# SwiGLU feed-forward on one core: three instead of four ordinary pairs of units ahead of the seven-product pairs, and a new order for the operands of the first of these

## The chip, the cores and the metric

One NeuronCore of a Trainium2 chip runs the whole program in one launch. The metric is the device time of that core in microseconds. The kernel before takes 2061.83 us, the median of three runs (2058.19 to 2067.65).

## What is computed

One inference step of a four-layer decoder trunk for 512 prompt tokens and 8 sample tokens, 520 columns in all. The layers have the mixers pool, conv, attention and pool, and each is followed by a feed-forward, which is where the change lies:

```python
def swiglu(h, w_gate, w_up, w_down):
    return (jax.nn.silu(h @ w_gate) * (h @ w_up)) @ w_down

xp = xp + swiglu(rmsnorm(xp, norm_ffn[i]), ffn_w_gate[i], ffn_w_up[i], ffn_w_down[i])
```

The model's width is 1024 (8 tiles of 128) and the feed-forward's 2816 (22 tiles of 128, numbered f). All is float32. The kernel computes each product as three: the operands are split into a high part (rounded to the engine's fp32r) and a low part (the rest), and hi\*hi + hi\*lo + lo\*hi are summed.

## The kernel before

Five engines run five programs written out by hand, in `@block.tensor`, `@block.scalar`, `@block.vector`, `@block.gpsimd` and `@block.sync`. Each goes through its own list in order; semaphores alone tie them together. There is no scheduler: the order of the Python code is the order on the engine. The gate weights of one f (128 columns of `w_gate`) and the up weights of the same f make a pair, and there are two ways to multiply it by the 520 tokens:

- **Ordinary** (`unit` on TensorE, the first PLAIN = 4 values of f of each layer, so 8 units). A unit is 8 input tiles by 2 token halves by 3 products, 48 matmuls of 260 columns, 96 for gate and up. Its weights are split by ScalarE (`split`, L1312, `w_hi`) and VectorE (`split`, L1817, `w_lo`). VectorE takes gate and up out of PSUM times `rstd` (L2009 `gate_n`, L2027 `up`), ScalarE takes silu (L1470), VectorE multiplies (L2036 `h`), and `h` is split too (`h_high` L1460, `h_low` L1999).
- **Seven-product** (`seven_blocks` on TensorE, L871, the other 18 values of f). Gate and up by the two halves of the inputs are a 2 by 2 matrix of blocks, and the halves of the inputs by the two halves of the tokens another; their product is made of seven block products instead of eight. A block is 4 input tiles by 3 products, 12 matmuls of 260 columns, 84 for a pair. It costs sums of operands: of weights on VectorE (`w_sum_2`, three sums, L1977 to L1980, and `w_sum_4`, one, L1988), each block's weights split (`high(j, b)` on ScalarE, L1455; `low(j, b)` on VectorE, L1994, 128x512 each), and, once a layer, sums and splits of the normed inputs: `scaled` (L1958, 16 instructions), four sums `xt` (L2025) and seven splits of 128x1040, `x_high(b)` (L1444) and `x_low(b)` (L1967), one for each block b of every pair. The results are joined (`join` on both engines): ScalarE copies the running bank out after blocks 0, 2 and 4 (L1502 `begun`), and TensorE must wait for the copies before blocks 2, 4 and 6, because these go on summing in the same bank (`pe.wait_ge(begun_ok, 3 * J + 1)` and so on; J counts pairs over the layers). VectorE adds the copies to other banks (L2057 to L2066), ScalarE takes silu of the halves (L1492, L1495), and VectorE makes `h` (L2070, L2071).

In the steady state the weights of pair j + 1 are split during pair j, and the first three sums of pair j + 2 are made after block 5 of pair j. The first pair has no pair before it: its operands, and the seven splits of the inputs, are made while TensorE is in the ordinary units. A layer runs the ordinary units, seven-product pairs up to f = 10, the first half of the down product, eleven more pairs, and the second half of it. SyncE loads weights into four places `raw`; a load waits until what lay there was split. On ScalarE and VectorE the loop `for c in range(PLAIN)` orders all this, and after it `join`. In ScalarE's `join(0)`:

```python
if b == 3:
    act.wait_ge(joined, 4 * J + 1)
    act.activation(silu2[:, 0:HALF], silu2[:, 0:HALF], ACT.Silu)
```

comes ahead of the copy after block 4, and so, in the same list, do the splits of the next pair's blocks 0 to 3 (`ahead(b)` stands behind each b).

Of the kernel before, what the change touches and what calls it, by code (L numbers as in the profile page):

```python
# [34 lines left out]
KT = D // P  # L35
# [17 lines left out]
PLAIN = 4  # L53
# [150 lines left out]
def trunk_step(nc, x_prompt, x_sample, state_pool, state_conv, cache_k, cache_v, page_table,  # L204
# [7 lines left out]
    with ctx:  # L212
# [1084 lines left out]
        def _(act):  # L1297
# [130 lines left out]
            def ffn(layer):  # L1428
# [32 lines left out]

                for c in range(PLAIN):
                    n, f = At(u + 2 * c), FT * layer + c
                    if c + 1 < PLAIN:
                        split(n + 2)
                    else:
                        for b in range(3):
                            high(0, b)
                    act.wait_ge(evacuated, m0 + 2 * c + 1)
                    act.activation(silu2[:], gate_n[:], ACT.Silu).then_inc(sg_ready, 1)  # L1470
                    if c + 1 < PLAIN:
                        split(n + 3)
                    else:
                        for b in (3, 4):
                            high(0, b)
                        x_high(4)
                        act.wait_ge(units_done, u + 2 * PLAIN)
                        for b in (5, 6):
                            x_high(b)
                            high(0, b)  # L1480
                    if c + 1 < PLAIN:
                        h_high(c)
                    for b in ((1, 2, 3) if c + 2 == PLAIN else (0,) if c + 3 == PLAIN else ()):
                        x_high(b)

                def join(j, ahead, last):

                    J, f = PAIRS * layer + j, PLAIN + j
                    for b in range(7):
                        if b == 3:  # L1490
                            act.wait_ge(joined, 4 * J + 1)
                            act.activation(silu2[:, 0:HALF], silu2[:, 0:HALF], ACT.Silu)  # L1492
# [3 lines left out]
                        act.wait_ge(blk_done, 7 * J + b + 1)  # L1496
                        if b in (0, 2, 4):
                            if J:
                                act.wait_ge(joined, 4 * J - 3 + b // 2)
                            if j == 0 and b == 0:  # L1500
                                act.wait_ge(sg_ready, FT * layer + PLAIN)
                            act.activation(begun[b // 2][:], pair[:, J % 2, 0:HALF], ACT.Copy).then_inc(begun_ok, 1)  # L1502
# [300 lines left out]
        def _(dve):  # L1803
# [142 lines left out]
            def ffn(layer):  # L1946
# [54 lines left out]
                for c in range(PLAIN):  # L2001
                    n, f = At(u + 2 * c), FT * layer + c
                    if c + 1 == PLAIN:
                        w_sum_2(0)
                        w_sum_4(0)
                    dve.wait_ge(units_done, n.start + 1)
                    if c:
                        dve.wait_ge(sg_ready, f)
                    dve.tensor_tensor(halves(gate_n[:]), accumulator(At(0)), halves(rstd[:]), ALU.mult).then_inc(evacuated, 1)  # L2009
                    if c + 1 < PLAIN:  # L2010
                        split(n + 2)
                    else:
                        for b in range(4):
                            low(0, b)
                    if c == 0:
                        for k in range(4):
                            scaled(k)
                    if c == 1:
                        dve.wait_ge(x_scaled, layer + 1)
                        dve.wait_ge(stored, 16 * STORED[("pool0", "conv", "attn", "pool1")[layer]])  # L2020
                        for to, a, b, made in ((xt[:, 0], xn1[:, 0:4], xn0[:, 0:4], 0), (xt[:, 1], xn1[:, 4:8], xt[:, 0], 1),
                                         (xt3[:], xn0[:, 4:8], xt[:, 1], 2), (xt[:, 2], xn1[:, 4:8], xn1[:, 0:4], 0)):
                            if made:
                                dve.wait_ge(x_summed, 4 * layer + made)
                            dve.tensor_tensor(to, a, b, ALU.subtract).then_inc(x_summed, 1)  # L2025
                    dve.wait_ge(units_done, n.start + 2)
                    dve.tensor_tensor(halves(up2[:]), accumulator(At(1)), halves(rstd[:]), ALU.mult).then_inc(evacuated, 1)  # L2027
                    if c + 1 == PLAIN:
                        low(0, 4)
                        x_low(4)  # L2030
                        for b in (5, 6):
                            x_low(b)
                            low(0, b)
                    dve.wait_ge(sg_ready, f + 1)
                    dve.wait_ge(evacuated, m0 + 2 * c + 2)
                    dve.tensor_tensor(h2[:], up2[:], silu2[:], ALU.mult).then_inc(h_ready, 1)  # L2036
                    if c + 1 < PLAIN:
                        split(n + 3)
                        h_low(c)
                    else:  # L2040
                        w_sum_2(1)
                    if c == 0:
                        for k in range(4, KT):
                            last = scaled(k)
                        last.then_inc(x_scaled, 1)
                    for b in ((1, 2, 3) if c + 2 == PLAIN else (0,) if c + 3 == PLAIN else ()):
                        x_low(b)
# [589 lines left out]
```

## Time and profile before

| | |
|---|---|
| median of three runs | 2061.83 us |
| the profiled execution, its own time | 2060.63 us |
| its span, first to last instruction | 2058.8 us |
| busy: TensorE, VectorE, ScalarE, GpSimd | 1999.7, 1414.7, 1055.4, 254.4 us |
| TensorE clock granted, mean | 0.995 of full |

The busy time of TensorE counts overlapped matmuls once. One matmul of 260 columns is shown with about 283 ns, but they are pipelined: the next starts about 120 ns after it, so work on TensorE is counted by starts. On VectorE and ScalarE too an instruction often starts a little before the one ahead has ended, and the step from start to start is what an instruction costs in a full queue.

### The profile page before, as it was taken

Reading aid. Unit: us, or ns where it says so; the run is one execution under the profiler, and the core shown is the slowest. Engines: PE = TensorE matmul, PEld = TensorE weight load, DVE = VectorE, ACT = ScalarE, POOL = GpSimd, SP = SyncE. Lnnn points to the kernel's source line nnn. Section 1 sums busy time; section 2 is a strip of 40 time slices with the busy share of each in tenths; the row PEclk is TensorE's granted clock in tenths of the full one; section 3 lists DMA queues with packets and bytes.
Section 4 is the critical chain, followed back from the end, with each engine's and each line's share of the span. In section 5 each row is a group of like instructions: output and inputs, shape, how many; then the busy total and the mean of one; then the engine's idle time right before and its main releaser. Section 6 shows DMA issues by size and latency. Waiting matters only on the chain.

```text
span 2058.8 us, 41713 instructions
## 1 busy us (share of the span) xinstructions
PE 1999.7 (97%) x16672; PEld 1933.2 (94%) x16672; DVE 1414.7 (69%) x2410; ACT 1055.4 (51%) x1842; POOL 254.4 (12%) x253
## 2 busy tenths in 40 slices
PE   8999999999899999999999979999999999999999
PEld 7999999997599999999999859999999999999999
DVE  5994696568768946964566655795597269937952
ACT  5553464465455534653777753463365355624642
POOL 4000000169320000001111124000000120000001
PEclk9999999999999999999999999999999999999999
DMA  6233333344222333333532342233333323333332
GB/s 187 74 103 97 98 104 100 89 119 119 64 73 72 103 93 102 103 98 95 177 114 82 108 180 84 84 83 99 96 108 99 109 62 87 97 92 110 103 97 79
DMA packets 350021, 208.22 MB, mean 101 GB/s; under 512 B 9897, under 2 KB 340553, under 8 KB 349812
## 3 DMA queue, kind: packets, MB, share of 16 engines
q1 hardware_dynamic: 345988, 198.26, 33.2%
q0 software_dynamic: 3472, 6.96, 1.0%
q8 instruction: 121, 1.98, 0.4%
q10 hardware_dynamic: 384, 0.55, 0.1%
q14 instruction: 56, 0.46, 0.1%
HBM read 194.53 MB, written 8.60 MB: 99 GB/s over the span
## 4 chain that ended last, share of the span: by engine, by line
PE 80%; DVE 9%; POOL 4%; issue 3%; ACT 3%; DMA 1%; SPq 0%; POOLq 0%; DVEq 0%; ACTq 0%
PE acc L671 41%; PE pair L871 19%; PE acc L871 9%; PE bank L871 4%; POOL conv L2540 4%; PE pair L1080 1%; DVE w_lo L1817 1%; PE bank L1100 1%; DMA hist_rows<-in_state_pool 1%; DVE w_lo L1994 1%; DVE xn L1958 1%; PE pair L1055 1%; DVE pair L2167 1%; ACT w_hi L1312 1%; DVE xt_lo L1967 1%
## 5 line engine op out<-in xcount | busy, mean ns | idle before, releaser
L1312 ACT ACTIVATE w_hi<-raw 128x768 fp32r<-128x768 f32 (+1 forms) x220 | 199.4, 906 | 439.3 <-PE acc L671 436.1
L671 PE MATMUL acc<-h_hi,w_hi 128*128 128x260 f32 x1408 | 399.0, 283 | 0.0
L671 PE MATMUL acc<-h_lo,w_hi 128*128 128x260 f32 x1408 | 398.3, 283 | 0.0
L671 PE MATMUL acc<-h_hi,w_lo 128*128 128x260 f32 x1408 | 397.7, 282 | 0.0
L1817 DVE TENSOR_TENSOR w_lo<-raw,w_hi 128x768 fp32r<-128x768 f32 (+1 forms) x220 | 241.9, 1099 | 216.3 <-ACT w_hi L1312 210.9
L671 PE MATMUL acc<-xin_hi,w_hi 128*128 128x260 f32 x1152 | 332.5, 289 | 6.0 <-DVE w_lo L1817 4.8
L671 PE MATMUL acc<-xin_hi,w_lo 128*128 128x260 f32 x1152 | 326.2, 283 | 0.0
L671 PE MATMUL acc<-xin_lo,w_hi 128*128 128x260 f32 x1152 | 325.7, 283 | 0.0
L671 PEld LDWEIGHTS acc<-h_hi,w_hi 128*128 128x128 f32 x1408 | 265.2, 188 | 0.3
L671 PEld LDWEIGHTS acc<-h_hi,w_lo 128*128 128x128 f32 x1408 | 265.1, 188 | 0.0
L671 PEld LDWEIGHTS acc<-h_lo,w_hi 128*128 128x128 f32 x1408 | 264.8, 188 | 0.0
L671 PEld LDWEIGHTS acc<-xin_hi,w_hi 128*128 128x128 f32 x1152 | 217.5, 189 | 20.5 <-issue 13.9
L671 PEld LDWEIGHTS acc<-xin_lo,w_hi 128*128 128x128 f32 x1152 | 217.6, 189 | 0.2
L671 PEld LDWEIGHTS acc<-xin_hi,w_lo 128*128 128x128 f32 x1152 | 217.5, 189 | 0.0
L1455 ACT ACTIVATE w_hi<-w_sum 128x512 fp32r<-128x512 f32 x216 | 132.8, 623 | 31.3 <-PE acc L871 20.5
L1994 DVE TENSOR_TENSOR w_lo<-w_sum,w_hi 128x512 fp32r<-128x512 f32 x216 | 147.3, 684 | 0.6
L1502 ACT ACTIVATE begun<-pair 128x260 f32<-128x260 f32 x216 | 82.8, 383 | 94.0 <-PE pair L871 93.0
L2452 POOL COPY sqacc<-sq 128x520 f32<-128x520 f32 x7 | 5.5, 782 | 961.2 <-ACT sq L1318 961.2
L1994 DVE TENSOR_TENSOR block<-raw,block 128x512 fp32r<-128x512 f32 x140 | 95.8, 687 | 39.2 <-ACT block L1455 38.5
L871 PE MATMUL pair<-xn_hi,block 128*128 128x260 f32 x576 | 114.9, 282 | 0.0
L871 PE MATMUL pair<-xt_hi,block 128*128 128x260 f32 x544 | 109.4, 284 | 0.0
L871 PE MATMUL bank<-xn_hi,block 128*128 128x260 f32 x544 | 109.2, 282 | 0.0
(445 smaller groups left out, 5264.9 us busy)
## 6 DMA issues: line engine op xcount, KB each, us to landing
raw<-in_ffn_w_gate SPq DMA_DIRECT2D x88, 512.0 KB, 4.0
raw<-in_ffn_w_up SPq DMA_DIRECT2D x88, 512.0 KB, 5.2
raw<-in_ffn_w_down SPq DMA_DIRECT2D x64, 384.0 KB, 3.5
raw<-in_ffn_w_down SPq DMA_DIRECT2D x64, 320.0 KB, 3.2
raw<-in_attn_w_qkv SPq DMA_DIRECT2D x24, 512.0 KB, 3.9
raw<-in_conv_w_in SPq DMA_DIRECT2D x16, 512.0 KB, 4.1
raw<-in_conv_w_out SPq DMA_DIRECT2D x8, 512.0 KB, 4.3
in_mix<-in_cache_k SPq DMA_DIRECT2D x8, 512.0 KB, 5.3
```

Of the source, the lines that this page charges most:

```text
L671: last = pe.matmul(acc[:, b, 0:HALF], w[:, w_tile * P:(w_tile + 1) * P], v[:, h * HALF:(h + 1) * HALF], start=start and t == 0, stop=stop ...
L871: last = pe.matmul(block_bank(J, b), w[:, cols], v[:, k, :], start=k + t == 0 and b in (0, 1, 3, 5), stop=k == 3 and t == 2, skip_group_ch ...
L1055: last = pe.matmul(pair[:, t, 0:HALF], blk, sq[:, 0, t * HALF:(t + 1) * HALF], start=True, stop=True)
L1080: last = pe.matmul(pair[:, c, off:off + w], qn[c * QK:(c + 1) * QK, i * P:(i + 1) * P], kn[c * QK:(c + 1) * QK, 0:w], start=True, stop=True)
L1100: last = pe.matmul(bank7[:, i * P:(i + 1) * P], aT[:, off + j * P:off + (j + 1) * P], v_tok[:, g % 2, j, :], start=j == 0, stop=j == i)
L1312: act.activation(w_hi[n.slot(2)][:, 0:cols], raw[:, q.slot(4), 0:cols], ACT.Copy).then_inc(split_hi, 1)
L1455: act.activation(block_w(j, b)[0], block_of(b, q), ACT.Copy).then_inc(blk_hi, 1)
L1502: act.activation(begun[b // 2][:], pair[:, J % 2, 0:HALF], ACT.Copy).then_inc(begun_ok, 1)
L1817: dve.tensor_tensor(w_lo[n.slot(2)][:, 0:cols], raw[:, raw_of(n).slot(4), 0:cols], w_hi[n.slot(2)][:, 0:cols].bitcast(F32), ALU.subtract). ...
L1958: last = dve.scalar_tensor_tensor(to[:, k, :], x[:, k, cols], g, rstd[:, cols], ALU.mult, ALU.mult)
L1994: dve.tensor_tensor(lo, block_of(b, raw_of_pair(layer, j)), hi.bitcast(F32), ALU.subtract).then_inc(blk_lo, 1)
L2540: pool_e.tensor_tensor(out, out, prod_p[:, p % 3, :], ALU.add).then_inc(prod_added, 1)
```

## The change

PLAIN becomes 3, so f = 3 is made by a seven-product pair too: 6 units, 8 pairs, down, 11 pairs, down. On VectorE and ScalarE the loop's conditionals are written out, and the operands of the first pair are made block by block: the input's split, the weights' split, then those of the next block. On ScalarE the copy of the bank after block 0 of the first pair is put ahead of the splits for blocks 5 and 6; in every pair silu of the first half moves from ahead of the copies of b = 3 to behind the copy after block 4. On VectorE the splits of the second pair's blocks 0 and 1 are made ahead of `join` rather than in it.

```diff
-PLAIN = 4
+PLAIN = 3
...
+                def copy_begun(J, b):
+
+                    act.wait_ge(blk_done, 7 * J + b + 1)
...
+                    act.activation(begun[b // 2][:], pair[:, J % 2, 0:HALF], ACT.Copy).then_inc(begun_ok, 1)
...
                     else:
-                        for b in range(3):
-                            high(0, b)
+                        x_high(0)
+                        high(0, 0)
                     act.wait_ge(evacuated, m0 + 2 * c + 1)
                     act.activation(silu2[:], gate_n[:], ACT.Silu).then_inc(sg_ready, 1)
...
+                x_high(1)
+                high(0, 1)
+                x_high(2)
+                high(0, 2)
+                x_high(3)
+                high(0, 3)
+                high(0, 4)
+                x_high(4)
+                act.wait_ge(units_done, u + 2 * PLAIN)
+                x_high(5)
+                copy_begun(PAIRS * layer, 0)
+                high(0, 5)
+                x_high(6)
+                high(0, 6)
...
                     for b in range(7):
-                        if b == 3:
-                            act.wait_ge(joined, 4 * J + 1)
-                            act.activation(silu2[:, 0:HALF], silu2[:, 0:HALF], ACT.Silu)
...
+                        if b == 4:
+                            act.wait_ge(joined, 4 * J + 1)
+                            act.activation(silu2[:, 0:HALF], silu2[:, 0:HALF], ACT.Silu)
...
+                gate_up(1, 1, up2)
+                h_of(1)
+                split(At(u + 5))
+                h_low(1)
+                x_low(0)
+                low(0, 0)
+                gate_up(2, 0, gate_n)
+                x_low(1)
+                low(0, 1)
+                w_sum_2(0)
+                x_low(2)
+                low(0, 2)
+                gate_up(2, 1, up2)
+                x_low(3)
+                low(0, 3)
+                w_sum_4(0)
+                x_low(4)
+                low(0, 4)
+                x_low(5)
+                low(0, 5)
+                h_of(2)
+                x_low(6)
+                low(0, 6)
+                low(1, 0)
+                low(1, 1)
+                w_sum_2(1)
...
-                            if not last:
+                            if not last and (j or b > 1):
                                 low(j + 1, b)
```

How the lists move, at the places that the prediction speaks of. The lines of the changed file are some numbers higher: in it L1976 is `x_low`, L2003 `low`, L2015 `gate_n` and `up`, L2021 `h`, L1986 to L1997 the sums of weights. The numbers behind names are the program's own: `block_83`, `early_86` and `early_87` hold the weights of blocks 0, 1 and 2, `w_lo_59` and `w_lo_60` of an ordinary unit or of blocks 3 and 4, 5 and 6; `xn_lo`, `xt_lo` and `late_lo` are the inputs' low parts.

VectorE in the first layer, the kernel before, from the first `x_low`:

```order
L1967 TENSOR_TENSOR xn_lo<-xn_79,xn_hi 128x1040
L2009 TENSOR_TENSOR gate_n<-acc,rstd 128x520
L1817 TENSOR_TENSOR w_lo_59<-raw,w_hi_57 128x1024
L2027 TENSOR_TENSOR up_101<-acc,rstd 128x520
L2036 TENSOR_TENSOR h_102<-up_101,silu_99 128x520
L1817 TENSOR_TENSOR w_lo_60<-raw,w_hi_58 128x1024
L1999 TENSOR_TENSOR h_lo<-h_102,h_hi 128x520
L1967 TENSOR_TENSOR xn_lo<-xn_79,xn_hi 128x1040
L1967 TENSOR_TENSOR xt_lo<-xt,xt_hi 128x1040 x2
L1977 TENSOR_TENSOR w_sum<-raw 128x512
L1978 TENSOR_TENSOR w_sum<-raw 128x512
L1980 TENSOR_TENSOR w_sum<-w_sum,raw 128x512
```

and the change, from the same place:

```order
L1976 TENSOR_TENSOR xn_lo<-xn_79,xn_hi 128x1040
L2003 TENSOR_TENSOR block_83<-raw,block_83 128x512
L2015 TENSOR_TENSOR gate_n<-acc,rstd 128x520
L1976 TENSOR_TENSOR xn_lo<-xn_79,xn_hi 128x1040
L2003 TENSOR_TENSOR early_86<-raw,early_86 128x512
L1986 TENSOR_TENSOR w_sum<-raw 128x512
L1987 TENSOR_TENSOR w_sum<-raw 128x512
L1989 TENSOR_TENSOR w_sum<-w_sum,raw 128x512
L1976 TENSOR_TENSOR xt_lo<-xt,xt_hi 128x1040
L2003 TENSOR_TENSOR early_87<-w_sum,early_87 128x512
L2015 TENSOR_TENSOR up_101<-acc,rstd 128x520
L1976 TENSOR_TENSOR xt_lo<-xt,xt_hi 128x1040
```

The two splits of ordinary weights have gone, and the first pair's operands begin right behind the first `x_low`.

VectorE at the start of the first `join`, the kernel before:

```order
L1994 TENSOR_TENSOR w_lo_60<-raw,w_hi_58 128x512
L2036 TENSOR_TENSOR h_102<-up_101,silu_99 128x520
L1977 TENSOR_TENSOR w_sum<-raw 128x512
L1978 TENSOR_TENSOR w_sum<-raw 128x512
L1980 TENSOR_TENSOR w_sum<-w_sum,raw 128x512
L1994 TENSOR_TENSOR block_83<-raw,block_83 128x512
L1988 TENSOR_TENSOR w_sum<-raw,w_sum 128x512
L2057 TENSOR_TENSOR silu_99<-bank,begun_95 128x260
```

and the change:

```order
L2003 TENSOR_TENSOR w_lo_60<-raw,w_hi_58 128x512
L2003 TENSOR_TENSOR block_83<-raw,block_83 128x512
L2003 TENSOR_TENSOR block_92<-raw,block_92 128x512
L1986 TENSOR_TENSOR w_sum<-raw 128x512
L1987 TENSOR_TENSOR w_sum<-raw 128x512
L1989 TENSOR_TENSOR w_sum<-w_sum,raw 128x512
L1997 TENSOR_TENSOR w_sum<-raw,w_sum 128x512
L2078 TENSOR_TENSOR silu_99<-bank,begun_95 128x260
```

The second pair's sums of weights now stand behind two of its splits.

ScalarE from the last ordinary silu to the first copy of the bank, before:

```order
L1470 ACTIVATE silu_99<-gate_n 128x520
L1455 ACTIVATE w_hi_57<-w_sum 128x512 x2
L1444 ACTIVATE xt_hi<-xt 128x1040
L1444 ACTIVATE late_hi<-xn_88 128x1040
L1455 ACTIVATE w_hi_58<-w_sum 128x512
L1444 ACTIVATE late_hi<-xt_89 128x1040
L1455 ACTIVATE w_hi_58<-raw 128x512
L1502 ACTIVATE begun_95<-pair 128x260
```

and the change:

```order
L1479 ACTIVATE silu_99<-gate_n 128x520
L1444 ACTIVATE xn_hi<-xn_79 128x1040
L1455 ACTIVATE early_86<-raw 128x512
L1444 ACTIVATE xt_hi<-xt 128x1040
L1455 ACTIVATE early_87<-w_sum 128x512
L1444 ACTIVATE xt_hi<-xt 128x1040
L1455 ACTIVATE w_hi_57<-w_sum 128x512 x2
L1444 ACTIVATE xt_hi<-xt 128x1040
L1444 ACTIVATE late_hi<-xn_88 128x1040
L1469 ACTIVATE begun_95<-pair 128x260
```

The copy is ahead of three splits that it followed, but four splits that were made before the last silu now stand behind it and ahead of the copy.

## Rows read from the trace of the kernel before

**Rows 1.** The page, part 1: busy time, share of the span and instructions.

```profile
PE 1999.7 (97%) x16672; PEld 1933.2 (94%) x16672; DVE 1414.7 (69%) x2410; ACT 1055.4 (51%) x1842; POOL 254.4 (12%) x253
```

**Rows 2.** TensorE's waits: us in total, times, longest us.

```profile
PE pair L871 <- ACT begun L1502: 13.7, 12, 1.6
```

**Rows 3.** The chain that ended last: start us, us, what.

```profile
1414.86 63.42 PE acc L671 x528
```

**Rows 4.** Timeline of TensorE, first layer: start us, us, what [idle before <-releaser].

```profile
77.94 0.39 PE L671 MATMUL acc<-xin_hi,w_hi 128*128 128x260 f32 x1 [0.78 <-DVE w_lo L1817]
...
95.28 0.28 PE L871 MATMUL pair<-xn_hi,block 128*128 128x260 f32 x1
...
99.83 0.39 PE L871 MATMUL pair<-xt_hi,early 128*128 128x260 f32 x1 [1.51 <-ACT begun L1502]
...
107.41 0.39 PE L871 MATMUL pair<-late_hi,w_hi 128*128 128x260 f32 x1 [1.55 <-ACT begun L1502]
...
115.25 0.38 PE L871 MATMUL pair<-xt_hi,w_hi 128*128 128x260 f32 x1 [0.39 <-ACT begun L1502]
```

**Rows 5.** Timeline of VectorE, first layer.

```profile
56.90 0.70 DVE L2009 TENSOR_TENSOR gate_n<-acc,rstd 128x520 f32<-128x520 f32 x1 [0.41 <-ACT rstd L1333]
...
78.41 1.24 DVE L1967 TENSOR_TENSOR xn_lo<-xn,xn_hi 128x1040 fp32r<-128x1040 f32 x1
79.57 0.69 DVE L2009 TENSOR_TENSOR gate_n<-acc,rstd 128x520 f32<-128x520 f32 x1
...
84.00 0.70 DVE L2027 TENSOR_TENSOR up<-acc,rstd 128x520 f32<-128x520 f32 x1 [2.61 <-PE acc L671]
...
90.64 0.69 DVE L1977 TENSOR_TENSOR w_sum<-raw 128x512 f32<-128x512 f32 x1
91.25 0.69 DVE L1978 TENSOR_TENSOR w_sum<-raw 128x512 f32<-128x512 f32 x1
...
103.88 0.69 DVE L1980 TENSOR_TENSOR w_sum<-w_sum,raw 128x512 f32<-128x512 f32 x1
```

**Rows 6.** Timeline of ScalarE, first layer.

```profile
80.30 0.64 ACT L1470 ACTIVATE silu<-gate_n 128x520 f32<-128x520 f32 x1 [0.97 <-DVE gate_n L2009]
...
87.05 2.02 ACT L1444 ACTIVATE xt_hi<-xt 128x1040 fp32r<-128x1040 f32 x2
...
99.42 0.36 ACT L1502 ACTIVATE begun<-pair 128x260 f32<-128x260 f32 x1
99.69 1.14 ACT L1455 ACTIVATE block<-raw 128x512 fp32r<-128x512 f32 x2
...
104.60 0.64 ACT L1455 ACTIVATE block<-w_sum 128x512 fp32r<-128x512 f32 x1 [1.17 <-DVE w_sum L1980]
```

**Rows 7.** Timelines, second and fourth layer: VectorE's first `gate_n`, TensorE's first block 6.

```profile
623.08 0.70 DVE L2009 TENSOR_TENSOR gate_n<-acc,rstd 128x520 f32<-128x520 f32 x1 [3.38 <-ACT rstd L1333]
...
674.66 0.39 PE L871 MATMUL pair<-late_hi,w_hi 128*128 128x260 f32 x1 [1.54 <-ACT begun L1502]
...
1699.10 0.70 DVE L2009 TENSOR_TENSOR gate_n<-acc,rstd 128x520 f32<-128x520 f32 x1 [3.02 <-ACT rstd L1333]
...
1749.51 0.39 PE L871 MATMUL pair<-late_hi,w_hi 128*128 128x260 f32 x1 [1.52 <-ACT begun L1502]
```

**Rows 8.** The page, part 6: a load's size in KB and median us to landing.

```profile
raw<-in_ffn_w_up SPq DMA_DIRECT2D x88, 512.0 KB, 5.2
```

**Rows 9.** Windows: us; busy of PE, PEld, DVE, ACT, POOL; PEclk, DMA share, GB/s.

```profile
242.00:340.00 98.00, 98.00 (x820) 98.00 (x819) 88.22 (x170) 61.94 (x124) 0.00 (x0) 1.00 0.37 102
...
484.00:487.40 3.40, 3.40 (x16) 3.40 (x17) 2.75 (x4) 1.66 (x3) 3.26 (x3) 0.50 0.38 89
487.40:490.80 3.40, 3.40 (x30) 3.40 (x29) 2.63 (x2) 1.52 (x3) 3.26 (x3) 0.99 0.67 178
```

**Rows 10.** Timeline of TensorE, conv mixer, ahead of the window at 484.00.

```profile
483.93 0.52 PE L671 MATMUL acc<-xin_hi,w_hi 128*128 128x260 f32 x1 [2.08 <-DVE w_lo L1817]
484.25 0.42 PE L671 MATMUL acc<-xin_lo,w_hi 128*128 128x260 f32 x1
484.46 0.42 PE L671 MATMUL acc<-xin_hi,w_lo 128*128 128x260 f32 x1
```

More of the change, by code:

```diff
@@ L1460, in h_high @@
                     act.activation(h_hi[:, f % FH, :], h2[:], ACT.Copy).then_inc(h_hi_ok, 1)
+                def copy_begun(J, b):
+                    act.wait_ge(blk_done, 7 * J + b + 1)
+                    if J:
+                        act.wait_ge(joined, 4 * J - 3 + b // 2)
+                    if J == PAIRS * layer and b == 0:
+                        act.wait_ge(sg_ready, FT * layer + PLAIN)
+                    act.activation(begun[b // 2][:], pair[:, J % 2, 0:HALF], ACT.Copy).then_inc(begun_ok, 1)
                 for c in range(PLAIN):
@@ L1472, in ffn @@
                         split(n + 3)
[L1473 to L1481, printed above, removed]
-                        h_high(c)
-                    for b in ((1, 2, 3) if c + 2 == PLAIN else (0,) if c + 3 == PLAIN else ()):
-                        x_high(b)
+                        h_high(c)
+                x_high(1)
[12 more added lines that the diff above has]
+                high(0, 6)
                 def join(j, ahead, last):
@@ L1495, in join @@
                             act.activation(silu2[:, HALF:T], silu2[:, HALF:T], ACT.Silu).then_inc(sg_ready, 1)
[L1496 to L1502, printed above, removed]
+                        if b in (0, 2, 4) and j + b:
+                            copy_begun(J, b)
+                        else:
+                            act.wait_ge(blk_done, 7 * J + b + 1)
+                        if b == 4:
+                            act.wait_ge(joined, 4 * J + 1)
+                            act.activation(silu2[:, 0:HALF], silu2[:, 0:HALF], ACT.Silu)
                         if b == (0 if j else 2) and j != PAIRS_OF[1][0]:
@@ L1999, in h_low @@
                     dve.tensor_tensor(h_lo[:, f % FH, :], h2[:], h_hi[:, f % FH, :].bitcast(F32), ALU.subtract).then_inc(h_lo_ok, 1)
[L2001 to L2034, printed above, removed]
@@ L2035, in ffn, with gate_up, h_of @@
+                def gate_up(c, j, to):
+                    dve.wait_ge(units_done, u + 2 * c + j + 1)
+                    if c and j == 0:
+                        dve.wait_ge(sg_ready, FT * layer + c)
+                    dve.tensor_tensor(halves(to[:]), accumulator(At(j)), halves(rstd[:]), ALU.mult).then_inc(evacuated, 1)
+                def h_of(c):
+                    dve.wait_ge(sg_ready, FT * layer + c + 1)
                     dve.wait_ge(evacuated, m0 + 2 * c + 2)
                     dve.tensor_tensor(h2[:], up2[:], silu2[:], ALU.mult).then_inc(h_ready, 1)
[L2037 to L2047, printed above, removed]
+                gate_up(0, 0, gate_n)
+                split(At(u + 2))
+                for k in range(4):
+                    scaled(k)
+                gate_up(0, 1, up2)
+                h_of(0)
@@ new lines, in ffn @@
+                split(At(u + 3))
+                h_low(0)
+                for k in range(4, KT):
+                    last = scaled(k)
+                last.then_inc(x_scaled, 1)
+                gate_up(1, 0, gate_n)
+                split(At(u + 4))
+                dve.wait_ge(x_scaled, layer + 1)
+                dve.wait_ge(stored, 16 * STORED[("pool0", "conv", "attn", "pool1")[layer]])
+                for to, a, b, made in ((xt[:, 0], xn1[:, 0:4], xn0[:, 0:4], 0), (xt[:, 1], xn1[:, 4:8], xt[:, 0], 1),
+                                 (xt3[:], xn0[:, 4:8], xt[:, 1], 2), (xt[:, 2], xn1[:, 4:8], xn1[:, 0:4], 0)):
+                    if made:
+                        dve.wait_ge(x_summed, 4 * layer + made)
+                    dve.tensor_tensor(to, a, b, ALU.subtract).then_inc(x_summed, 1)
```

## The prediction

> **What bounds the kernel now.** I read the page first: TensorE is busy 97% of the span [rows 1], so a change counts by what it does to TensorE's list. Then TensorE's waits: the longest line is twelve waits for `begun`, 13.7 us [rows 2], three in the first pair or two of each of the four layers. The chain gives TensorE's pace: 528 matmuls in 63.42 us, 0.12 us each [rows 3], so a block is 1.44 us, an ordinary pair 96 x 0.12 = 11.5 us and a seven-product pair 84 x 0.12 = 10.1 us.
>
> TensorE's timeline in the first layer shows what the three waits cost [rows 4]. Block 0 starts at 95.28; two blocks end the pace at 98.16, and block 2 starts at 99.83: 1.7 us lost. Four blocks later it would be at 105.7 (the first matmul after a wait takes 0.1 more); block 6 starts at 107.41: 1.7 us. Five blocks later it would be at 114.7; block 4 of the second pair starts at 115.25: 0.5 us. No other wait follows in the feed-forward.
>
> The releaser that the trace names is ScalarE's copy, 0.36 us of work. But behind it is VectorE. From the first `gate_n` at 56.90 to the sums of the second pair's weights at 103.88 its list has one real hole, 2.61 us ahead of the `up` at 84.00, where it waited for TensorE [rows 5]. ScalarE, which copies in list order, sat idle 1.17 us for those same sums before it could go on to the third copy [rows 6]. So the start of each feed-forward is a race: VectorE must have all operands of the first pair, and the first sums of the second, by the time that TensorE is through the ordinary units and six blocks. VectorE loses it by some 3.4 us.
>
> **What the change takes away.** One ordinary pair becomes a seven-product pair: 12 matmuls less in a layer, 4 x 12 x 0.12 = **5.8 us** off TensorE. That is sure.
>
> **What it does to the race.** TensorE comes to block 0 two units, 11.5 us, sooner. VectorE is spared ahead of it one `gate_n`, one `up`, one `h`, one `h_low` and two splits of 128x1024: about 4.7 us at the steps of its list (0.61 for 520 columns, some 1.14 for 1024). The rest of 6.8 us must come from the hole of 2.61 us or be waited for. The new list can be laid on the clock of the first layer. Steps from start to start: a split or sum of 512 columns 0.60 (90.64 to 91.25), one of 1040 columns 1.16 (78.41 to 79.57) [rows 5]; on ScalarE 0.64 for a silu or its like, 0.96 for 1040 columns (two in 2.02) and 0.52 for 512 (two in 1.14) [rows 6].
>
> - Up to the first `x_low` at 78.41 nothing moves. Then one weights' split at 79.57 and `gate_n` at 80.17, ready at 80.9.
> - The next `x_low` now waits for ScalarE, which takes the silu of that `gate_n` first (0.64) and then copies the input (1.06): it starts at **82.5**. So the list has a new hole of 1.8 us in the place of the old one: the block order makes VectorE wait for ScalarE where the old order had other work.
> - From there to the third sum of the second pair's weights: six `x_low` (6.9), eight weights' splits (4.8), four sums for the first pair and three for the second (4.2), `up` and `h` (1.2) are 17.2 us: **99.8**.
> - ScalarE then makes two splits of 512 columns and the copy, 0.52 + 0.52 + 0.36: block 6 of the first pair starts at **101.3**. Here the move of silu pays: before, 107.41 was 2.8 us behind the end of the sum at 104.6, now it is 1.5.
>
> TensorE's own list: the last ordinary unit starts at 77.94 as before and waits as before [rows 4]; 5.86 us later, at 83.8, comes block 0, and without waits block 6 would be due at 92.4. So it stands for some 8.9 us in its first pair instead of 3.4: about 4.4 us ahead of block 2 (the first pair's third sum is done at 86.2, and ScalarE has three inputs, three weights' splits and the copy ahead, 4.8 us, so 91.1), 0.3 ahead of block 4, 3.9 ahead of block 6, and then 0.8 instead of 0.5 in the second pair.
>
> The sum goes by block 6, counted from the first `gate_n` at 56.90. Now it is 50.5 us behind it, after the change 44.4: 6.1 us sooner. But behind it lies one more pair, 10.1 us, and 0.3 us more of the third wait: **+4.2 us**. The fourth layer is the same, 1749.51 less 1699.10, 50.4: +4.3. In the second 674.66 less 623.08 is 51.6 [rows 7], TensorE being later there and VectorE's time unchanged: 7.2 sooner, so **+3.2**; the third layer has the second's distances: +3.1. Together +14.8 us; the 5.8 us saved are in it, set against some 20.6 us of standing.
>
> The second half of each layer (eleven pairs) and the down products have the same lists as now: nothing. In the steady state VectorE is busy 88.22 of 98 us [rows 9]; silu's later place is covered by that tenth, and the missing work would come out as waits like the third if it were not. Loads: the third pair's weights go out when the first pair's last split is done, 96.8, and are wanted at 104.8; 8 us cover a landing of 5.2 [rows 8].
>
> **The clock.** A stand of TensorE can cost more than its length. The eight stands of 1.7 us left the clock full. After one of 2.08 us idle [rows 10] it fell to the lower level, 1.2 GHz, and for 3.4 us there were 16 matmuls in the place of some 28 at the full one [rows 9]: 12 x 0.12, 1.5 us lost. The new stands of 3.4 to 4.4 us are long enough to bring this. After the first one it costs nothing: blocks 2 to 5 only eat into the stand ahead of block 6. After that stand up to 1.5 us are lost, of which the third wait gives 0.8 back. I take 0.4 us a layer, between nothing and 0.7: +1.6 us. The ends are 0 and 4 x 1.5 = 6 us.
> The Trainium skill ("TensorE: Matmul & The Clock Gate", section "Why this matters for your kernels") advises against idle gaps of TensorE between bursts, since the clock then drops; it speaks against this change.
>
> **Forecast.** 2060.63 (the profiled execution, 1.2 us under the median of 2061.83) + 14.8 + 1.6 = **2077.0 us**, 0.75% slower. A difference under 0.5%, 10.3 us, is about what a measurement of this kernel can't tell from none.
>
> **Rivals.**
> - *The order is what was missing* (the other side). The trace names ScalarE's copy as releaser; if the copies come early enough the stands end, which gives 4 x (1.44 + 1.7 + 1.7 + 0.5 + 0.3) = 22.6 us: **2038**. It decides by whether VectorE has the second pair's third sum by the end of block 5, 92.4. For it: the copy after block 0 passes two splits. Against it: VectorE's list gives 99.8, and no order shortens a full list. Chance 0.03.
> - *Stands as they are*, only the matmuls saved: 2060.63 - 5.8 = **2055**, the same by the bound. VectorE would have to find 5.7 us more room a layer. 0.05. Half way, where the new hole of 1.8 us a layer doesn't open, 2060.63 + 14.8 - 7.2 = **2068**: 0.04.
> - *The backlog stays*: the third wait's 0.8 us comes in five more pairs of each layer, +16: **2093**. Against it, VectorE's spare tenth is 1 us a pair. 0.04.
> - *The slow clock is paid in full*, at both long stands of each layer, 8 x 1.5 = 12 us in place of 1.6: **2087**. Against it, the second stand hides the first fall. 0.04. By the skill's advice read strictly, each long stand would be paid so.
> - The forecast's mechanism: 0.80.
>
> The range is 2068 (no new hole, no slow clock) to 2085 (14.8 + 6 for the clock + 3.2 for one more wait of 0.8 in each layer). Slower: 0.80 + 0.04 + 0.04 and none of the others, 0.88; same: 0.05 + 0.04, 0.09; faster 0.03.
>
> **What would show it.** Right: TensorE's waits for `begun` grow from 13.7 to over 30 us; ahead of block 2 some 4.4 us in the first and fourth layer and 3.4 in the others, ahead of block 6 between 2.4 and 3.9 (less where the clock was low before it); VectorE's `x_low` with a hole of 1.8 us ahead of it that ScalarE ends, and no other hole up to the second pair's sums; block 6 about 44.4 us behind the first `gate_n` in every layer; the lower clock for a few us in the first pair. Wrong: block 6 earlier than 41 us behind `gate_n`, stands that begin in later pairs, or waits for a load.

## The result and the profile after

The changed kernel takes 2082.13 us, the median of five runs (2076.13 to 2083.48), against 2062.67 for five runs of the kernel before (2058.19 to 2067.76): 1.0078 times as long, 95% interval 1.0057 to 1.0098, so 12 to 20 us slower. The forecast was 2077.0 in a range of 2068 to 2085, slower.

The profiled execution took 2082.66 us, its span is 2080.9 (before 2058.8, so 22.1 more), its mean clock 0.984 of full (before 0.995). Part 1 of its page, which answers to [rows 1]:

```profile
PE 2013.3 (97%) x16624; PEld 1945.8 (94%) x16624; DVE 1432.3 (69%) x2458; ACT 1068.2 (51%) x1878; POOL 253.9 (12%) x253
```

There are 48 matmuls less, four times 12, and yet TensorE is "busy" 13.6 us more: at the lower clock matmuls start about 0.21 us apart instead of 0.12 (this kernel's blocks 2 to 5), and each is shown longer. Its waits, answering to [rows 2] (us in total, times, longest):

```profile
PE pair L871 <- ACT begun L1469: 24.6, 10, 4.3
```

L1469 is `copy_begun`, the old L1502. TensorE's timeline in the first and second layer shows where these waits are, in the place of [rows 4] (start us, us, what, idle before and its releaser):

```profile
87.93 0.28 PE L871 MATMUL pair<-xn_hi,block 128*128 128x260 f32 x1
...
95.22 0.58 PE L871 MATMUL pair<-xt_hi,early 128*128 128x260 f32 x1 [4.25 <-ACT begun L1469]
...
105.42 0.58 PE L871 MATMUL pair<-late_hi,w_hi 128*128 128x260 f32 x1 [2.67 <-ACT begun L1469]
...
179.04 0.36 PE L671 MATMUL acc<-h_hi,w_hi 128*128 128x260 f32 x1
...
666.16 0.59 PE L871 MATMUL pair<-xt_hi,early 128*128 128x260 f32 x1 [3.43 <-ACT begun L1469]
...
676.36 0.39 PE L871 MATMUL pair<-late_hi,w_hi 128*128 128x260 f32 x1 [1.54 <-ACT begun L1469]
...
684.51 0.39 PE L871 MATMUL pair<-xt_hi,w_hi 128*128 128x260 f32 x1 [0.65 <-ACT begun L1469]
```

The first three are blocks 0, 2 and 6 of the first pair; 179.04 is the first matmul of the down product. The last three are the second layer's blocks 2 and 6 and block 4 of its second pair. VectorE's timeline, first layer, from its first `gate_n` to the second pair's third sum, in the place of [rows 5]:

```profile
61.04 0.70 DVE L2015 TENSOR_TENSOR gate_n<-acc,rstd 128x520 f32<-128x520 f32 x1 [0.41 <-ACT rstd L1333]
...
84.31 0.69 DVE L2015 TENSOR_TENSOR gate_n<-acc,rstd 128x520 f32<-128x520 f32 x1
86.67 1.24 DVE L1976 TENSOR_TENSOR xn_lo<-xn,xn_hi 128x1040 fp32r<-128x1040 f32 x1 [1.67 <-ACT xn_hi L1444]
...
98.46 0.68 DVE L2021 TENSOR_TENSOR h<-up,silu 128x520 f32<-128x520 f32 x1
...
103.24 0.68 DVE L1989 TENSOR_TENSOR w_sum<-w_sum,raw 128x512 f32<-128x512 f32 x1
```

The hole before the second `x_low` is there, and behind it no row up to the sum at 103.24 shows idle time. ScalarE's timeline, in the place of [rows 6]:

```profile
85.03 0.64 ACT L1479 ACTIVATE silu<-gate_n 128x520 f32<-128x520 f32 x1 [2.00 <-DVE gate_n L2015]
85.58 1.06 ACT L1444 ACTIVATE xn_hi<-xn 128x1040 fp32r<-128x1040 f32 x1
...
94.81 0.36 ACT L1469 ACTIVATE begun<-pair 128x260 f32<-128x260 f32 x1
...
103.95 0.63 ACT L1455 ACTIVATE block<-w_sum 128x512 fp32r<-128x512 f32 x1 [4.13 <-DVE w_sum L1989]
104.48 0.61 ACT L1455 ACTIVATE w_hi<-w_sum 128x512 fp32r<-128x512 f32 x1
105.00 0.37 ACT L1469 ACTIVATE begun<-pair 128x260 f32<-128x260 f32 x1
```

ScalarE takes silu and one input (1.6 us) while VectorE waits for that input; later ScalarE itself waits 4.13 us for VectorE's third sum, and the copy that lets TensorE into block 6 at 105.42 stands behind it.

**Where the 22.1 us lie.** Read from the first `gate_n` of a layer to the first matmul of its down product, start to start. In the first layer that is 170.04 - 56.90 = 113.1 us before and 179.04 - 61.04 = 118.0 after; the four layers were 113.1, 114.2, 114.2 and 113.1, and are 118.0, 117.7, 117.4 and 117.9: together **16.3 us more**. The first `gate_n` of all starts 4.1 us later (61.04 against 56.90), and the rest lies outside the feed-forwards' first halves, nearly all of it (1.8 us) between the second layer's down product and the third layer's first `gate_n`, where the attention mixer is. The 4.1 us are not the change's, which touches nothing ahead of that point: in e3 below, with the same code up to there, it starts at 54.99. The windows of the same stretch (PEclk is the third column from the end; first the kernel after, then before) show what it is:

```profile
20.10:33.70 13.60, 13.60 (x66) 13.55 (x65) 5.71 (x13) 3.22 (x6) 0.00 (x0) 0.50 0.64 209
```

```profile
20.10:33.70 13.60, 13.60 (x105) 13.04 (x104) 6.53 (x14) 5.67 (x10) 1.46 (x2) 0.89 0.73 233
```

In this execution the clock stayed at 0.50, its lower level of 1.2 GHz, for the whole stretch: 66 matmuls instead of 105, and 39 x 0.12 = 4.7 us. Other profiled executions have it or not, whatever the kernel (below).

### The profile page after: what moved, and what is told of

It is laid out like the page before. It is cut to its first block and busy times, and to the rows that moved or that the text cites. A ratio compares the mean times of both kernels' runs of the same rounds, so it can differ in the third digit from the quotient of the medians.

```text
span 2080.9 us, 41765 instructions
## 1 busy us (share of the span) xinstructions
PE 2013.3 (97%) x16624; PEld 1945.8 (94%) x16624; DVE 1432.3 (69%) x2458; ACT 1068.2 (51%) x1878; POOL 253.9 (12%) x253
## 5 line engine op out<-in xcount | busy, mean ns | idle before, releaser
L1312 ACT ACTIVATE w_hi<-raw 128x768 fp32r<-128x768 f32 (+1 forms) x212 | 190.8, 900 | 420.1 <-PE acc L671 417.2
L1826 DVE TENSOR_TENSOR w_lo<-raw,w_hi 128x768 fp32r<-128x768 f32 (+1 forms) x212 | 232.0, 1094 | 216.0 <-ACT w_hi L1312 210.4
L671 PE MATMUL acc<-xin_hi,w_hi 128*128 128x260 f32 x1024 | 296.4, 289 | 6.0 <-DVE w_lo L1826 4.8
L671 PE MATMUL acc<-xin_hi,w_lo 128*128 128x260 f32 x1024 | 290.1, 283 | 0.0
L671 PE MATMUL acc<-xin_lo,w_hi 128*128 128x260 f32 x1024 | 289.6, 283 | 0.0
L671 PEld LDWEIGHTS acc<-xin_hi,w_hi 128*128 128x128 f32 x1024 | 193.4, 189 | 20.5 <-issue 13.9
L671 PEld LDWEIGHTS acc<-xin_lo,w_hi 128*128 128x128 f32 x1024 | 193.5, 189 | 0.2
L671 PEld LDWEIGHTS acc<-xin_hi,w_lo 128*128 128x128 f32 x1024 | 193.4, 189 | 0.0
L1455 ACT ACTIVATE w_hi<-w_sum 128x512 fp32r<-128x512 f32 x228 | 142.0, 628 | 47.6 <-PE acc L871 36.6
L1469 ACT ACTIVATE begun<-pair 128x260 f32<-128x260 f32 x228 | 87.8, 385 | 137.8 <-PE pair L871 134.6
L2003 DVE TENSOR_TENSOR w_lo<-w_sum,w_hi 128x512 fp32r<-128x512 f32 x228 | 155.2, 682 | 1.3 <-ACT w_hi L1455 1.3
L2003 DVE TENSOR_TENSOR block<-raw,block 128x512 fp32r<-128x512 f32 x148 | 100.9, 686 | 42.0 <-ACT block L1455 39.9
```

The source lines that it names most:

```text
L671: last = pe.matmul(acc[:, b, 0:HALF], w[:, w_tile * P:(w_tile + 1) * P], v[:, h * HALF:(h + 1) * HALF], start=start and t == 0, stop=stop ...
L1312: act.activation(w_hi[n.slot(2)][:, 0:cols], raw[:, q.slot(4), 0:cols], ACT.Copy).then_inc(split_hi, 1)
L1455: act.activation(block_w(j, b)[0], block_of(b, q), ACT.Copy).then_inc(blk_hi, 1)
L1826: dve.tensor_tensor(w_lo[n.slot(2)][:, 0:cols], raw[:, raw_of(n).slot(4), 0:cols], w_hi[n.slot(2)][:, 0:cols].bitcast(F32), ALU.subtract). ...
L2003: dve.tensor_tensor(lo, block_of(b, raw_of_pair(layer, j)), hi.bitcast(F32), ALU.subtract).then_inc(blk_lo, 1)
```

## The experiments

Three theories. **R**: VectorE's list sets when block 6 of the first pair can start; ScalarE's copy is only the last link. **C**: the time hangs on ScalarE's copies, which the trace names as releasers. **O**: what the changed kernel has of use is the block-wise order, and fewer ordinary pairs need it. All kernels were measured beside the kernel before; ratios are to it. Its own median was 2062.67 beside the changed kernel, 2061.71 beside e1 to e4, 2061.13 beside e5 and e6 and 2066.67 beside e7 and e8, so between kernels of different sets ratios are safer than medians, and the feed-forwards, where the edits lie, are safer than both. The last columns are from the profiled execution: start of the first pair's block 6 behind the layer's first `gate_n` (second layer), and `gate_n` to the down product, four layers added, less the 454.7 us of before.

| kernel | median us | ratio and 95% interval | block 6 | four feed-forwards |
|---|---|---|---|---|
| before | 2062.67 | 1 | 51.6 | 0 |
| changed | 2082.13 | 1.0078 (1.0057 to 1.0098) | 44.7 | +16.3 |
| e1, old order | 2068.11 | 1.0028 (1.0014 to 1.0041) | 42.8 | +7.7 |
| e2, copies alone | 2061.97 | 1.0001 (0.9984 to 1.0018) | 50.2 | +0.1 |
| e3, hole filled | 2075.17 | 1.0057 (1.0041 to 1.0072) | 42.9 | +12.0 |
| e4, short `x_low` | 2061.92 | 0.9992 (0.9973 to 1.0011) | 40.6, no wait | -1.9 |
| e5, four, filled | 2052.84 | 0.9966 (0.9952 to 0.9979) | 49.5 | -8.5 |
| e6, and `h` later | 2050.26 | 0.9945 (0.9932 to 0.9959) | 48.9, no wait | -12.1 |
| e7, filled, sums first | 2070.17 | 1.0031 (1.0014 to 1.0048) | 41.7 | +7.5 |
| e8, copies back | 2075.83 | 1.0050 (1.0033 to 1.0068) | 45.6 | +15.2 |

**Three ordinary pairs, the old order (e1).** Besides PLAIN, one line on either engine puts the input splits of blocks 0 to 3 together, behind the second ordinary pair (shown for ScalarE); all else is as before.

```diff
-PLAIN = 4
+PLAIN = 3
...
-                    for b in ((1, 2, 3) if c + 2 == PLAIN else (0,) if c + 3 == PLAIN else ()):
+                    for b in range(4) if c + 2 == PLAIN else ():
```

Expected:

> Three ordinary pairs with the old grouping of the lists (the first input split joins the other three behind the second h_low; nothing else of the new order). Theory R (the race: VectorE's full list sets the start of block 6): the old list has no wait for ScalarE in its middle, so it is through 1.8 us earlier than the changed one in each layer; first gate_n to the first down product 4 x 1.8 us shorter than in the changed kernel, in all about +8 us against the kernel before (2071), with a new stand of 2 to 3 us ahead of block 0. Theory O (the new order is what helps): without it the loss is larger than the change's, over +20 us (over 2083).

Measured: 2068.11 us, R's figure less 3. O falls: with the old order the kernel is 14 us faster than with the new one, 8.6 of them in the feed-forwards. VectorE has no hole here, as its list from the first `x_low` on shows:

```profile
82.48 2.39 DVE L1967 TENSOR_TENSOR xn_lo<-xn,xn_hi 128x1040 fp32r<-128x1040 f32 x2
84.79 2.39 DVE L1967 TENSOR_TENSOR xt_lo<-xt,xt_hi 128x1040 fp32r<-128x1040 f32 x2
87.10 0.68 DVE L1977 TENSOR_TENSOR w_sum<-raw 128x512 f32<-128x512 f32 x1
```

TensorE waits ahead of block 0 instead, for VectorE by name, and ahead of block 6 again:

```profile
90.97 0.58 PE L871 MATMUL pair<-xn_hi,block 128*128 128x260 f32 x1 [2.96 <-DVE block L1994]
...
103.85 0.39 PE L871 MATMUL pair<-late_hi,w_hi 128*128 128x260 f32 x1 [1.26 <-ACT begun L1502]
```

These are the first layer's rows; in the second and third it stands 1.8 us ahead of block 0 and 2.2 ahead of block 2. Block 6 is at 103.85 - 60.97 = 42.9 us behind `gate_n`, 1.5 before the changed kernel's 44.4, which is about the hole. Going to three ordinary pairs thus costs 6 to 8 us, and the rest of the change about as much again (16.3 - 7.7 = 8.6 in the feed-forwards).

**The copies moved up, four ordinary pairs (e2).**

```diff
                             x_high(b)
+                            if b == 5:
+                                copy_begun(PAIRS * layer, 0)
                             high(0, b)
...
-                        if b == 3:
+                        if b == 4:
                             act.wait_ge(joined, 4 * J + 1)
                             act.activation(silu2[:, 0:HALF], silu2[:, 0:HALF], ACT.Silu)
```

The second piece also moves behind the copy.

> Four ordinary pairs, only ScalarE's copies moved as in the change (the copy after block 0 ahead of the splits for blocks 5 and 6, silu of the first half behind the copy after block 4). Theory R: the stand ahead of block 2 (1.7 us) goes, and as much comes back ahead of block 6 and in the second pair: the same time as before within 2 us. Theory C (ScalarE's copy, which the trace names as releaser, is the cause): the stands go for good, 3.4 to 4.2 us a layer, 2046 to 2049.

Measured: no difference, 1.0001. Block 6 of the first pair does come sooner, by 1.4 us in each layer (50.2 against 51.6 behind `gate_n` in the second), since the wait ahead of block 2 has gone. But the down product does not: +0.1 us in all. In the first and fourth layer two waits in the second pair, 0.78 and 0.65 us, took the place of one of 0.39, each for a copy that stands behind VectorE's work; in the second and third the lower clock took the gain. The first and fourth, where the clock stayed full, thus speak for R by themselves. TensorE's timeline, first and second layer, and the windows behind block 6:

```profile
103.44 0.39 PE L871 MATMUL pair<-late_hi,w_hi 128*128 128x260 f32 x1 [1.79 <-ACT begun L1469]
...
108.80 0.39 PE L871 MATMUL pair<-xt_hi,block 128*128 128x260 f32 x1 [0.78 <-ACT begun L1469]
...
112.62 0.39 PE L871 MATMUL pair<-xt_hi,w_hi 128*128 128x260 f32 x1 [0.65 <-ACT begun L1469]
...
669.52 0.48 PE L871 MATMUL pair<-late_hi,w_hi 128*128 128x260 f32 x1 [1.79 <-ACT begun L1469]
```

```profile
103.44:106.84 3.40, 3.40 (x28) 3.40 (x29) 3.40 (x8) 1.47 (x3) 0.00 (x0) 1.00 0.29 73
669.70:673.10 3.40, 3.40 (x17) 3.40 (x18) 3.40 (x7) 1.35 (x3) 0.00 (x0) 0.50 0.25 60
```

The same idle time of 1.79 us was followed by the full clock once and by the lower one once. C falls: the releaser that the trace names was moved, and what came of it at block 6 was gone a pair later, VectorE's list being as full as before.

**The hole filled (e3).** The first pair's three sums, which need no input, go ahead of the `x_low` that waits.

```diff
                 gate_up(2, 0, gate_n)
+                w_sum_2(0)
                 x_low(1)
                 low(0, 1)
-                w_sum_2(0)
```

> The changed kernel with the first pair's three weight sums ahead of the second input split on VectorE, in the place where it waits for ScalarE. Theory R: VectorE's new hole of 1.8 us closes, block 6 starts 1.8 us earlier in each layer (42.6 us behind the first gate_n in place of 44.4), 7 us less than the changed kernel, +8 us against the kernel before. Theory C: nothing of the third copy's place changes, so the same time as the changed kernel.

Measured: 2075.17, 7.0 us under the changed kernel by the medians, but 4.3 us (16.3 - 12.0) in the feed-forwards of the profiled executions. That the medians give just R's figure is chance in part. VectorE's hole has gone, and block 6 comes 1.75 us sooner in each layer, 7.0 in all, as R said. The trace tells why the feed-forwards did not get all of it: blocks 2 to 5 now run earlier and mostly at full clock, so TensorE's stand ahead of block 6 grew, and in every layer the lower clock followed it (in the changed kernel in the first and fourth alone).

```profile
97.62 0.39 PE L871 MATMUL pair<-late_hi,w_hi 128*128 128x260 f32 x1 [3.74 <-ACT begun L1469]
...
667.08 0.58 PE L871 MATMUL pair<-late_hi,w_hi 128*128 128x260 f32 x1 [3.74 <-ACT begun L1469]
```

```profile
97.62:101.02 3.40, 3.40 (x21) 3.40 (x22) 3.40 (x8) 1.64 (x5) 0.00 (x0) 0.71 0.11 27
667.08:670.48 3.40, 3.40 (x15) 3.40 (x16) 3.40 (x8) 1.62 (x5) 0.00 (x0) 0.50 0.12 28
670.48:673.88 3.40, 3.40 (x22) 3.40 (x22) 3.31 (x7) 1.65 (x5) 0.00 (x0) 0.71 0.00 0
```

**VectorE's list cut (e4).** `x_low` subtracts 8 of each 260 columns instead of all, and TensorE reads the high part in its place: the same instructions, but about 1.05 us less for each of seven on VectorE in a layer (a duration of 0.19 instead of 1.24).

```diff
-                        for t, (w, v) in enumerate(((hi, x_hi), (hi, x_lo), (lo, x_hi))):
+                        for t, (w, v) in enumerate(((hi, x_hi), (hi, x_hi), (lo, x_hi))):
...
-                    dve.tensor_tensor(lo, own, hi.bitcast(F32), ALU.subtract).then_inc(xs_lo_ok, 1)
+                    few = slice(0, 8)
+                    dve.tensor_tensor(lo[:, :, few], own[:, :, few], hi.bitcast(F32)[:, :, few], ALU.subtract).then_inc(xs_lo_ok, 1)
```

> The changed kernel with VectorE's seven input splits cut to 8 of 260 columns each (128x32 in place of 128x1040); TensorE multiplies by the inputs' high part twice and not by the low part, so its list and ScalarE's are of the same length. It leaves the low parts of the inputs out. Theory R: VectorE's list is 6.4 us shorter ahead of block 6; the stands shrink from 9.2 us to about 5.2 (3.2 ahead of block 2, which ScalarE's list then sets, 0.9 ahead of block 6) and the time is 15 to 17 us less than the changed kernel, about 2060. Theory C: ScalarE's list is as it was, so the stands stay: the same as the changed kernel.

Measured: 2061.92, 20 us under the changed kernel, 18.2 of them in the feed-forwards, where R had 15 to 17, with ScalarE's list untouched. It leaves out the inputs' low parts, so it is a probe and no kernel to use, but it is the plainest evidence for R. The waits for the copies fell with it, from 24.6 to 12.5 us:

```profile
PE pair L871 <- ACT begun L1469: 12.5, 8, 3.0
```

The wait ahead of block 6 is no more; what is left stands mostly ahead of block 2, where ScalarE's list is the bound.

**Four ordinary pairs, lists written out, hole filled (e5).** The old kernel too has a hole on VectorE, the 2.61 us of [rows 5]. Here it is filled with the second and third input splits, `x_low(1)` and `x_low(2)`. The core of the edit, on VectorE:

```diff
-PLAIN = 3
+PLAIN = 4
...
                 gate_up(2, 0, gate_n)
+                split(At(u + 6))
                 x_low(1)
...
                 x_low(2)
...
                 gate_up(2, 1, up2)
+                h_of(2)
+                split(At(u + 7))
+                h_low(2)
                 x_low(3)
...
+                w_sum_2(0)
                 w_sum_4(0)
...
-                low(1, 0)
-                low(1, 1)
                 w_sum_2(1)
```

ScalarE makes the high parts in the matching order, and its copies stand where they did before.

> Four ordinary pairs; both lists written out so that VectorE has other work where it waited for TensorE ahead of the third up (2.6 us): the second and third input split stand there, ScalarE makes their high parts earlier, and the weights' splits of the first pair stand ahead of the last gate_n. Theory R: VectorE is through 2.1 us earlier in each layer; the stands in the first two pairs sum to 1.7 us in place of 3.9, 8.5 us less than the kernel before (2054). Theory C (copies on ScalarE): the copies stand where they stood, so no change. A third possibility, that the order counts for nothing because the loads set it: no change either, with waits for landings in VectorE's list.

Measured: 2052.84, faster than both kernels (0.9966). Block 6 comes 2.1 us sooner in each layer and the feed-forwards are 8.5 us shorter, both as R said. Only lists were reordered, with the same loads, so the third possibility falls with C. In place of the row at 84.00 VectorE's `up` now finds nearly no hole in the first layer, 0.2 us between 79.88 + 1.16 and 81.25 (in the second and third 1.1 are left, of 3.4 before):

```profile
79.88 1.23 DVE L1978 TENSOR_TENSOR xt_lo<-xt,xt_hi 128x1040 fp32r<-128x1040 f32 x1
81.25 0.70 DVE L2017 TENSOR_TENSOR up<-acc,rstd 128x520 f32<-128x520 f32 x1
```

**And `h` later (e6).** Silu of the first half behind the copy after block 4, and the split of `h` behind block 2 in every pair, on both engines.

```diff
-                        if b == 3:
+                        if b == 4:
                             act.wait_ge(joined, 4 * J + 1)
                             act.activation(silu2[:, 0:HALF], silu2[:, 0:HALF], ACT.Silu)
-                        if b == (0 if j else 2) and j != PAIRS_OF[1][0]:
+                        if b == 2 and j != PAIRS_OF[1][0]:
                             h_high(f - 1)
...
+                            dve.wait_ge(h_ready, FT * layer + f)
                             dve.tensor_tensor(silu2[:, 0:HALF], gate_0, begun[0][:], ALU.add).then_inc(joined, 1)
```

As in e2, the first piece also goes behind the copy. The added wait is for VectorE's own `h`, made earlier in its list.

> As the last, and in every pair silu of the first half behind the copy after block 4 and the split of h behind block 2 on both engines, so that the copy after block 2 of the second pair doesn't wait for h. Theory R: the wait in the second pair (0.5 us a layer) goes too: 12 us less than the kernel before (2050 to 2051), stands of about 0.9 us a layer left.

Measured: 2050.26, 0.9945 times the kernel before, **11 us faster than it and 32 faster than the changed kernel** (12.1 and 28.4 in the feed-forwards; R had 12). TensorE's waits of [rows 2], 13.7 us, are down to

```profile
PE pair L871 <- ACT begun L1510: 2.2, 4, 0.6
```

**The hole filled and the second pair's sums first (e7).** On top of e3:

```diff
+                w_sum_2(1)
                 low(1, 0)
                 low(1, 1)
-                w_sum_2(1)
```

> The changed kernel with its hole filled, and VectorE's sums of the second pair's weights put back ahead of the splits of that pair's blocks 0 and 1 (1.2 us of work that the change moved in front of them). Theory R (VectorE's list sets when block 6 of the first pair can start): block 6 comes 1.2 us sooner in each layer than in the run with the hole filled alone (+41.4 instead of +42.6 us behind the first gate_n), so 4.8 us less in all: 5 us under that run, 12 us under the changed kernel, some 3 us (0.15%) over the kernel before. Theory C (the time hangs on ScalarE's copies): no difference from the run with the hole filled alone.

Measured: 2070.17, 5.0 us under e3, and 1.0031, the old order's figure within the interval. Block 6 comes 1.2 us sooner in every layer (41.7 against 42.9 in the second), as R said, and the four feed-forwards are 4.5 us shorter. So of the changed kernel's 16.3 us, 4.3 go with the hole (e3) and 4.5 with the place of these sums. The 7.5 that are left are e1's 7.7: the block-wise order, with its copies moved up, brings nothing over the old one.

**The changed kernel with the copies back (e8).**

```diff
                 x_high(5)
-                copy_begun(PAIRS * layer, 0)
                 high(0, 5)
                 x_high(6)
                 high(0, 6)
+                copy_begun(PAIRS * layer, 0)
...
+                        if b == 3:
+                            act.wait_ge(joined, 4 * J + 1)
+                            act.activation(silu2[:, 0:HALF], silu2[:, 0:HALF], ACT.Silu)
...
-                        if b == 4:
-                            act.wait_ge(joined, 4 * J + 1)
-                            act.activation(silu2[:, 0:HALF], silu2[:, 0:HALF], ACT.Silu)
```

> The changed kernel with ScalarE's copies where they were before: the copy after block 0 of the first pair behind the splits for blocks 5 and 6 (2.0 us later), silu of the first half ahead of b = 3. Theory R: the stand ahead of block 2 becomes 2.0 us longer and the one ahead of block 6 shorter by as much; block 6 itself comes only 0.3 us later, behind silu. 1 to 2 us over the changed kernel in all. Theory C: each of the 2.0 us counts, 8 us over the changed kernel (0.4%).

Measured: 2075.83, below the changed kernel's median by 6, though the two intervals overlap; in the feed-forwards it is 1.1 us shorter. C's 8 us more are out. R had the stands right and the sum wrong by 2 to 3 us. TensorE, first layer:

```profile
91.62 0.58 PE L871 MATMUL pair<-xt_hi,early 128*128 128x260 f32 x1 [6.53 <-ACT begun L1469]
...
100.45 0.38 PE L871 MATMUL pair<-late_hi,w_hi 128*128 128x260 f32 x1 [0.60 <-ACT begun L1469]
```

Ahead of block 2 it stands 2.3 us longer, ahead of block 6 2.1 shorter. Block 6 is 0.9 us later rather than 0.3: silu of the first half waits for VectorE's join, as ScalarE's row shows, and the copy behind it waits too.

```profile
99.18 0.42 ACT L1504 ACTIVATE silu<-silu 128x260 f32<-128x260 f32 x1 [0.49 <-DVE silu L2078]
```

From first to last start blocks 2 to 5 took 99.57 - 91.62 = 7.95 us, partly at the lower clock, instead of 5.75 in the kernel before, and TensorE still came early to block 6. The short stand there left the clock full behind it, where the changed kernel lost some 1.5 us in two layers. So by the trace the later silu is worth 0.9 us at block 6, and the earlier copy turned one long stand into two and won nothing. Both moves were undone together, so how the two share in the 1.1 us is not shown.

## Why the prediction was right, point by point

- **What bounds it.** The start of each feed-forward is a race that VectorE's list loses, with the copy as the last link: shown by e2 and e8 (copies moved, no lasting gain) against e3, e4, e5 and e7 (VectorE's list changed, the gain follows).
- **Matmuls.** 48 less, 5.8 us, as counted.
- **Block 6.** Forecast 44.4 us behind the first `gate_n`; measured 44.4, 44.7, 44.3 and 44.3. **The hole** of 1.8 us: 1.67 idle. Laid on the clock of before, `x_low` was to start at 82.5; the layer began 4.14 us later, so 86.6, and it started at 86.67. **Block 2**: 34.2 us behind `gate_n` forecast (91.1 - 56.9), 34.2 measured.
- **The stands.** Ahead of block 2, 4.4 and in the second and third layer 3.4 forecast; idle 4.25 and 4.26, and 3.43 and 3.10. The third wait of 0.8 came in the second and third layer (gap of 0.94 less a matmul's 0.12), but not in the first and fourth, and the 0.3 ahead of block 4 in none: the lower clock in blocks 2 to 5, or behind block 6, covered them.
- **A miss in the signs to look for.** "TensorE's waits for `begun` grow from 13.7 to over 30 us": they are 24.6. The text itself said that the lower clock would eat into the stand ahead of block 6, and that total did not take it off. That stand was to be 2.4 to 3.9; it was 2.67 and 2.64 in the first and fourth layer and 1.54 and 1.40 in the others, where the lower clock lasted through some 26 of the 48 matmuls of blocks 2 to 5, against some 15.
- **The sum.** +14.8 and 1.6 for the clock, 16.4; measured 16.3 in the four feed-forwards, +4.9, +3.5, +3.1 and +4.8. (Redone from the prediction's own rows, 10.1 + 0.3 a layer less 6.1, 7.2, 7.2 and 6.0 is 15.0, not 14.8.) The clock's 1.6 is thus right in total, and unequally spread: from block 6 to the down product there are 72.0 us of matmuls, and the stretch took 1.6 us more than that in the first and fourth layer and 1.0 in the others, where 1.2 was forecast for each (the 0.4 of the clock and the third wait's 0.8). No layer had the 0.4: in two the clock fell behind block 6, which cost 1.5 us and spared the third wait, in two it did not fall there. That the mean comes out is luck in part.
- **The rest.** The profiled execution is 22.0 us slower than that of before, not 16.4: 4.1 are the slow start, 1.6 the mixers. Both medians probably mix executions with and without it (last section), and 16.4 us lies inside the interval of the ratio (12 to 20).
- **The rivals.** "The hole doesn't open", priced at 2068, was tried as e3 and gave 2075: the step that failed in that price is the clock, since a stand of 3.7 us ahead of block 6 brought the lower level in every layer. The old order (e1), which has no hole and shorter stands, gave 2068.1.

The Trainium skill ("TensorE: Matmul & The Clock Gate", section "Why this matters for your kernels") advises against idle gaps between bursts. The runs agree: behind the 3.74 us of idle in e3 the clock fell in all four layers. They add that such a fall is free where TensorE comes to its next stand anyway: in e8 blocks 2 to 5 at the lower clock cost nothing, since block 6 was not due.

## What to carry to other kernels

The releaser that a trace names is the last link: follow it back until you reach an engine whose list has no idle time, and count that list from a fixed point. A new order pays only if it leaves no hole in that engine's list; put work that depends on nothing into each place where it would wait, and what others wait for ahead of what they do not. Time at the lower clock costs nothing where the work done in it ends in a wait anyway.

## What had not been expected of the hardware

- **The start of an execution is not always the same.** Of the ten profiled executions three (the changed kernel, e1, e4) spent most or all of the stretch from 20.1 to 33.7 us at the lower clock, the one of before a part of it, and the other six none. That is 4 to 6 us, and of the size of the two groups in which the changed kernel's five runs fall (2076.1 and 2076.9; 2082.1, 2082.7 and 2083.5); the profiled one, with the slow start, is in the upper group. The mean granted clock of each run goes with the groups, 0.988 and 0.989 in the lower and 0.984 to 0.985 in the upper; 13.6 us at half the clock would lower the mean by 0.003. Where in the unprofiled runs the clock was low is not shown. A difference of 0.3% between single runs says nothing here.
- **Idle times of 1.8 to 2.5 us are undecided.** In e2 one of 1.8 left the clock full in two layers and was followed by the lower level in two. In e7 TensorE was idle 2.52 and 2.54 us ahead of block 6 in the first and second layer; the windows behind it:

```profile
97.09:100.49 3.40, 3.40 (x16) 3.40 (x17) 3.40 (x8) 1.46 (x3) 0.00 (x0) 0.52 0.54 138
664.71:668.11 3.40, 3.40 (x28) 3.40 (x29) 3.40 (x8) 1.47 (x3) 0.00 (x0) 1.00 0.59 150
```

The prediction took the waits of 1.5 us idle, 1.7 lost, as safe, and no feed-forward here shows a fall behind one; it took 2.08 idle [rows 10] as bringing a fall, and that is no rule.
